# An encoder block with two head groups on one core: the fourth tile of x turned by VectorE's blocks and a trip over DRAM

## What is computed

```python
h = rmsnorm(x, norm_mix[l])                       # x: (1, 1024, 1024)
proj = jnp.einsum('bsd,dc->bsc', h, w_in[l])
qa, ka, va, ga, cq, ckv, kr, gb = jnp.split(proj, split_idx, axis=-1)
...
q = jnp.einsum('bsc,ce->bse', rmsnorm(cq, q_a_norm[l]), w_uq[l])
kv = jnp.einsum('bsc,ce->bse', rmsnorm(ckv, kv_a_norm[l]), w_ukv[l])
k_rope = apply_rope(kr.reshape(B, S, 1, B_ROPE), cos, sin)[:, :, 0, :]
```

## Time and profile before

| | us |
|---|---|
| median of 3 runs | 606.72 (605.74 to 607.55) |
| the profiled execution | 606.28 |
| its span in the trace | 604.4 |
| PE busy | 595.3 (98% of the span) |
| DVE busy | 446.4 (74%) |
| ACT busy | 356.3 (59%) |
| POOL busy | 292.4 (48%) |
| DMA queue of SP | 101.25 MB, 56.2% of 16 engines' span |
| granted clock of TensorE | full in all slices but the last |

### The profile page before, as it was taken

One profiled execution on the slowest core, in us unless ns is written; L12 is line 12 of the kernel. 1 busy time (PEld: TensorE's weight loads), 2 busy tenths in 40 slices (PEclk: granted clock), 3 DMA queues, 4 the chain that ended last, 5 costly groups with the idle time before them and its releaser, 6 DMA issues.

```text
span 604.4 us, 9197 instructions
## 1 busy us (share of the span) xinstructions
PE 595.3 (98%) x3076; PEld 484.0 (80%) x3076; DVE 446.4 (74%) x802; ACT 356.3 (59%) x762; POOL 292.4 (48%) x273
## 2 busy tenths in 40 slices
PE   8999999999999999999999999999999999999996
PEld 7888888788888888888887777777777777888885
DVE  5777663334434439898899788998998988799884
ACT  6644223213333228777787678788788788524563
POOL 4610702515656532536556537677677776510601
PEclk9999999999999999999999999999999999999998
DMA  7587457774776720101015967767768745598042
GB/s 246 190 287 203 155 166 242 230 259 149 245 262 226 224 69 1 36 1 36 2 27 114 242 157 185 190 179 191 192 172 199 203 127 182 177 386 326 1 173 107
DMA packets 72431, 102.11 MB, mean 169 GB/s; under 512 B 10232, under 2 KB 43008, under 8 KB 72384
## 3 DMA queue, kind: packets, MB, share of 16 engines
q1 hardware_dynamic: 72224, 101.25, 56.2%
q10 hardware_dynamic: 160, 0.27, 0.1%
HBM read 60.17 MB, written 31.62 MB: 152 GB/s over the span
## 4 chain that ended last, share of the span: by engine, by line
PE 78%; DMA 8%; DVE 5%; ACT 3%; POOL 2%; SPq 2%; issue 1%; ACTq 0%; DVEq 0%
PE ps L1824 13%; PE ps L1826 13%; PE ps L1825 13%; PE ps L2118 9%; PE ps L2096 7%; PE ps L2026 5%; PE ps L2031 5%; PE ps L1996 3%; PE ps L2046 2%; DMA lat_scratch<-lat_b 2%; PE ps L2006 2%; DMA lat<-lat_scratch 2%; PE ps L1983 2%; PE ps L1982 2%; PE ps L2007 2%; DMA ukv_raw<-w_ukv 1%
## 5 line engine op out<-in xcount | busy, mean ns | idle before, releaser
L1674 DVE TENSOR_TENSOR pT_lo<-ps,pT_hi 128x512 fp32r<-128x512 f32 x102 | 69.3, 684 | 21.5 <-ACT pT_hi L1237 20.3
L1824 PE MATMUL ps<-hT_hi,w_hi 128*128 128x512 f32 x208 | 84.0, 404 | 0.0
L1826 PE MATMUL ps<-hT_hi,w_lo 128*128 128x512 f32 x208 | 81.4, 391 | 0.0
L1825 PE MATMUL ps<-hT_lo,w_hi 128*128 128x512 f32 x208 | 81.1, 390 | 0.0
L1224 ACT ACTIVATE p_b<-ps,stat 128x1024 f32<-128x1024 f32 x64 | 71.3, 1114 | 12.6 <-DVE stat L1649 12.2
L1649 DVE TENSOR_REDUCE stat<-ps 128x1 f32<-128x1024 f32 x64 | 76.5, 1212 | 2.2 <-PE ps L2046 2.0
L1237 ACT ACTIVATE pT_hi<-ps 128x512 fp32r<-128x512 f32 x102 | 60.4, 596 | 23.8 <-PE ps L2096 23.5
L2096 PEld LDWEIGHTS ps<-ident,p_b 128*128 128x128 f32 x408 | 48.7, 140 | 17.4 <-issue 5.2
L2096 PE MATMUL ps<-ident,p_b 128*128 128x128 f32 x408 | 62.0, 275 | 0.6 <-DVE pT_lo L1674 0.3
L810 POOL TENSOR_SCALAR p_w<-p_w,stat 128x384 f32<-128x384 f32 (+1 forms) x40 | 24.4, 623 | 55.7 <-DVE stat L1557 55.7
L926 POOL TENSOR_TENSOR pT_lo<-p_land,pT_hi 128x512 fp32r<-128x512 f32 x26 | 33.3, 1286 | 29.5 <-ACT pT_hi L1244 29.5
(11 more groups left out here) (222 smaller groups left out, 1506.2 us busy)
## 6 DMA issues: line engine op xcount, KB each, us to landing
w_raw<-w_in SPq DMA_DIRECT2D x13, 512.0 KB, 4.5
probs_scratch<-p_blk SPq DMA_DIRECT2D x52, 128.0 KB, 2.8
p_land<-probs_scratch SPq DMA_DIRECT2D x13, 512.0 KB, 4.2
x_in<-x SPq DMA_DIRECT2D x8, 512.0 KB, 3.8
wt_raw<-w_out SPq DMA_DIRECT2D x8, 512.0 KB, 4.4
t_scratch<-wt_hi SPq DMA_DIRECT2D x16, 256.0 KB, 2.6
t_scratch<-wt_lo SPq DMA_DIRECT2D x16, 256.0 KB, 2.8
q<-q_h SPq DMA_DIRECT2D x16, 256.0 KB, 3.7
```

Of the source, the lines that this page charges most:

```text
L1674: nc.vector.tensor_tensor(pT_lo[at_], ps[:, 4 + a, :].rearrange("p (k c) -> p k c", c=P), f(pT_hi[at_]), ALU.subtract).then_inc(s_bTl, 1)
L1824: nc.tensor.matmul(o, a_hi, b_hi, start=first, stop=False, skip_group_check=goes_on)
L1825: nc.tensor.matmul(o, a_hi, b_lo, start=False, stop=False, skip_group_check=goes_on)
L1826: return nc.tensor.matmul(o, a_lo, b_hi, start=False, stop=last, skip_group_check=goes_on)
```

## The change

- `X_PE` goes from 4 to 3: tile 3 is no longer turned on TensorE but by `turn_blocks(3)`, `store_x(3)` and `fetch_x(3)`, and lands in `latT_hi[:, 4, :]`. `turn_x(3)` leaves TensorE's program.
- The buffers alternate by t % 2, so tile 3 writes `x_blk1`, and tiles 4 and 6 `x_blk0`. `x_blk0` moves from 147 KB (where `lat` lies) to 201 KB. `lat_norm(0)` no longer waits until the blocks of an x tile are stored, and `lat_norm(1)` waits for those of tile 7 (`x_blk1` lies where `lat_b1` does) as before, counted anew.
- ScalarE: `h_hi(3)` stands behind the last weight split, ahead of `square_x(6)`; `h_hi(4)` ahead of `lat_stats(0)`.
- VectorE: `h_lo(3)` stands behind `turn_blocks(5)` (before: behind `turn_blocks(4)`); `h_lo(4)` ahead of `lat_norm(0)` (before: behind it).
- SP: `store_x(3)` ahead of `load_x(6)`; `g_q` and `g_kv` behind `load_x(6)`; `fetch_x(3)` ahead of `store_x(4)`; `fetch_x(4)` ahead of `store_x(5)`.

```diff
-X_PE = 4
+X_PE = 3
...
-        x_blk = [at(f"x_blk{i}", kb, [P, 4, KT, Q32]) for i, kb in enumerate((147, 161))]
+        x_blk = [at(f"x_blk{i}", kb, [P, 4, KT, Q32]) for i, kb in enumerate((201, 161))]
...
         def x_turned(t):
-            a, r = ((latT_hi, 0), (latT_hi, 2), (latT_lo, 0), (latT_lo, 2))[t - X_PE]
+            if t == X_PE:
+                return f(latT_hi[:, 4, :]).rearrange("p (r c) -> p r c", r=2)
+            a, r = ((latT_hi, 0), (latT_hi, 2), (latT_lo, 0), (latT_lo, 2))[t - X_PE - 1]
...
+            store_x(3)
             load_x(6)
+            sp.dma_start(g_q[:, :], q_a_norm.partition_broadcast(P)).then_inc(s_glat, 16)
+            sp.dma_start(g_kv[:, :], kv_a_norm.partition_broadcast(P)).then_inc(s_glat, 16)
+            fetch_x(3)
             store_x(4)
             load_x(7)
+            fetch_x(4)
             store_x(5)
-            fetch_x(4)
             store_x(6)
             fetch_x(5)
             store_x(7)
...
             square_x(4)
-            h_hi(3)
             wn_hi_k(6)
             square_x(5)
             wn_hi_k(7)
+            h_hi(3)
             square_x(6)
             square_x(7)
+            h_hi(4)
             lat_stats(0)
-            h_hi(4)
...
                     lat_lo(t - 2)
                     dve.wait_ge(s_latT, t - 1)
-                else:
-                    dve.wait_ge(s_xsto[t], 128)
+                elif t == 1:
+                    dve.wait_ge(s_xsto[1], 192)
...
             for t in range(X_PE, NT):
                 norm_x(t)
                 turn_blocks(t)
-                if t == 4:
+                if t == 5:
                     h_lo(3)
+            h_lo(4)
             lat_norm(0)
-            h_lo(4)
...
             both(2, range(4))
-            turn_x(3)
```

More of the change, by code:

```diff
@@ L236, in encoder @@
         s_wnh, s_wnr = sem("wn_hi_ready"), sem("wn_ready")
-        s_grow, s_gcol, s_gT, s_gb = sem("g_row_in"), sem("g_col_ready"), sem("g_turned"), sem("g_broadcast")
+        s_grow, s_gcol, s_gT, s_gb = sem("g_row_then_fourth_tile_in"), sem("g_col_ready"), sem("g_turned"), sem("g_broadcast")
         s_pA, s_pB = sem("natA_done"), sem("natB_done")
@@ L438, in _ @@
             load_wn(7)
-            sp.dma_start(g_q[:, :], q_a_norm.partition_broadcast(P)).then_inc(s_glat, 16)
-            sp.dma_start(g_kv[:, :], kv_a_norm.partition_broadcast(P)).then_inc(s_glat, 16)
             def store_x(t):
@@ L450, in fetch_x @@
                 sp.dma_start(x_turned(t), xt_scr[t - X_PE].rearrange("a p (r q) c -> (a p) r (q c)", r=2)) \
-                    .then_inc(s_xq[t - X_PE], 16)
+                    .then_inc(s_xq[t - X_PE - 1] if t > X_PE else s_grow, 16)
+            store_x(3)
             load_x(6)
+            sp.dma_start(g_q[:, :], q_a_norm.partition_broadcast(P)).then_inc(s_glat, 16)
+            sp.dma_start(g_kv[:, :], kv_a_norm.partition_broadcast(P)).then_inc(s_glat, 16)
+            fetch_x(3)
             store_x(4)
             load_x(7)
+            fetch_x(4)
             store_x(5)
-            fetch_x(4)
             store_x(6)
@@ L1000, in h_hi @@
                 if t >= X_PE:
-                    act.wait_ge(s_xq[t - X_PE], 16)
+                    act.wait_ge(s_xq[t - X_PE - 1], 16) if t > X_PE else act.wait_ge(s_grow, 32)
                     for r in range(2):
@@ L1443, in _ @@
             h_lo(0, range(1, 2))
-            for t in range(1, 4):
+            for t in range(1, X_PE):
                 norm_x(t)
-                if t < 3:
-                    h_lo(t)
+                h_lo(t)
             def turn_blocks(t):
```

## The result

| | before | after |
|---|---|---|
| median of 6 runs, us | 606.57 (605.42 to 607.55) | 612.33 (609.09 to 614.05) |
| ratio, 95% interval | | 1.0097 (1.0074 to 1.0121) |
| the profiled execution, us | 606.28 | 609.09 |
| its span | 604.4 | 607.2 |
| its mean granted clock | | 0.998 |

What follows compares the result with a forecast made beforehand. Up to 109 us TensorE's work and the DMA-trip chain were taken as nearly equal bounds. The chain starting 3.3 us later, 2.8 carried less 0.25 slack, added 2.5 to 606.28; forecast 609.0, range 606.0 to 611.3.

Steps and rivals of the forecast that it cites:

- the bound: Up to 109 us, TensorE's work and the DMA-trip chain nearly equal; the chain has almost no slack.
- the direction: Whole kernel slower, 609.0 us forecast; chance of slower by more than 0.3% put at 0.54.
- TensorE's 0.80 us: turn_x(3) removed from TensorE's path: natural(3) could start at 38.4, 0.80 earlier; most eaten by a wait before natural(4).
- T3: Landing of tile 3's trip (store, then fetch): 36.1 us, between 34.8 and 37.5.
- T3 + 10.7 = 46.8: Reciprocal of lat_norm(0), after ScalarE's and VectorE's work behind tile 3's landing: 46.8 instead of 43.51, 3.3 us later.
- Rival 3: Waits pile up as turn_blocks(7) waits for tile 5's stores behind fetch_x(4): 611.3 us, decides from T3 above 37; 14 in 100.
- the carry: First latents to job 8: delay of 2.05 to 3.3, taken as 2.8, less 0.25 slack, 2.5 us at job 8.
- The sum: Whole kernel: 606.28 + 2.5 = 608.8 us profiled, 609.2 on the median, given as 609.0.
- 0.7 ahead of `natural(4)`: TensorE waits 0.7 us until lat_norm(0) has read its banks at 47.9, eating most of the 0.80 saved.
- some 2.5 us more at job 8: TensorE's added wait at job 8 for the late chain, with nothing beyond the existing wait at the k jobs.

Runs made afterwards that it cites:

- the trip made and not used: Changed kernel making all of tile 3's trip, while TensorE turns tile 3 again and h_hi(3), h_lo(3) read PSUM at their old places; 610.97 us, 1.0063.
- both orders taken back: Changed kernel with fetch_x(4) back behind store_x(5) and tile 6's square, norm and blocks ahead of tile 3's hi and lo parts; 609.27 us, 1.0049.
- the two put-in waits: Kernel before with four, or two, copies on VectorE ahead of the last latT_lo, so TensorE waits at job 8; 610.46 us (1.0053) and 607.08 us (1.0008).
- their filled one: Kernel before with the four VectorE copies, TensorE filling the wait at job 8 with 28 turns of the identity; 608.40 us, 1.0032.
- x_blk0's place: Kernel before with only x_blk0 moved to 201 KB and lat_norm(0)'s wait for tile 6's stores removed; 606.05 us, 1.0001.
- the fifth tile's order: Kernel before with only h_hi(4) put ahead of lat_stats(0) and h_lo(4) ahead of lat_norm(0); 607.51 us, 1.0011.
- the two filled kernels: Changed kernel with TensorE's two new waits filled by unread transposes, 610.73 us (1.0063); kernel before with its four-copy wait filled likewise, 608.40 us (1.0032).
- the kernel with its waits filled: Changed kernel, TensorE filling its new waits with identity transposes, 14 inside natural(3) and 24 ahead of job 8; 610.73 us, 1.0063.

## Why the prediction was right or wrong

**Right: the bound and the direction.** TensorE's 0.80 us bought nothing, the chain of DMA trips set the end of the first sixth, and the change made it later. That the profiled execution, at 609.09, lies beside the forecast of 609.0 is luck: its job 8 came 3.9 later and not 2.5, it took back 1.1 of this by the end of the span, and it is the one run of six whose mean clock shows no fall.

**Almost right: T3.** 36.87 for 36.1, inside its 34.8 to 37.5. The stores landed at 31.11 (forecast 30.9), the fetch took 5.7 us (5.2). The estimate from the figures of the Trainium skill ("DMA: Bandwidth & Descriptors", section on the anatomy of one DMA), 32.3, is 4.6 us too early; that section's fit is for DMAs issued by GpSimd, and here SP issues them. `natural(3)` saved 0.32 of 0.80. The prediction saw no wait for it; `hT_lo(3)` ends at 37.53 + 1.29 = 38.82, so it could not have started before, but TensorE had by then lost 0.37 to the late split of the last weights and waited for `hT_lo(3)` less than 0.1.

**The step that failed: the first latents, T3 + 10.7 = 46.8, "the chain starts 3.3 us later".** They came at 48.22, and the chain started 4.7 later. With the measured T3 the step gives 47.6. It assumed that VectorE's row of work is the only path. Rival 3 had named the other one (`turn_blocks(7)` behind the stores of tile 5, held by `fetch_x(4)`), gave it 14 in 100, and put its threshold at a T3 above 37. It decided already at 36.87. Its stores were under-costed: 5.0 to 5.7 us each, where tile 4's take 6.8 from the first issue (31.50) to the landing (38.27), with tile 3's fetch and the load of tile 7 in flight, and tile 5's 6.1. In the changed kernel these two paths end within a microsecond of each other (VectorE would be free for `turn_blocks(7)` at 44.33, the stores have landed at 45.11), so taking one away can bring back a microsecond at most. A third path was not in the prediction at all: the load of tile 7 takes 6.0 us in the changed kernel and 7.5 with the trip made and not used, for 4.5 before. It decides only with both orders taken back.

**Right in its amount by luck, wrong in its steps: the carry, "2.05 to 3.3, I take 2.8", less 0.25.** The forecast let 0.8 us of the delay go on the way to job 8 (3.3 to 2.5), and 0.8 went (4.7 to 3.9). So job 8 is 1.4 later than forecast because the chain started 1.4 later. But the steps were others. The forecast took off 0.5 because `lat_norm(1)` loses less, and it did (+3.5 where `lat_norm(0)` has +4.7). But the chain goes by tile 0: its fetch, its `latT_lo` (57.90, +4.7 by 53.17) and so the latents of tile 2. The earlier trace rows had shown it, with the fetch of tile 0 followed by the store of tile 2. The store of tile 6's latents is still issued 4.7 later (86.89 by 82.18). The 0.8 goes behind it, where the forecast had 0.25, and 0.7 of it because the latents of tiles 6 and 7 happened to land faster than before (3.7 us from the first issue to the fetch that waits, for 4.2, and 3.7 for 4.0). w_ukv was issued at 96.62 and not at 95.3, the first k job came 3.45 later. From the first reciprocal to job 8 the kernel before takes 52.85 us; the ten others with the same chain (all of the table but the two put-in waits and their filled one) take 52.1 to 54.3, 53.4 in the mean. A start that is 0.9 earlier is lost in this scatter of 2 us, and so is what one path taken away may bring back at job 8: with one execution each, job 8 doesn't order the variants.

**Missing: a term for the clock.** The sum turned waits of TensorE into microseconds one for one. The waits of 1.7 and 2.2 us were forecast in kind (0.7 ahead of `natural(4)`, "some 2.5 us more at job 8"), but a wait like these can bring the granted clock to 0.50 shortly after TensorE resumes, at 1.7 us in each of the six falls that profiled executions show. Clocks of 0.996 or less, which no run of before, of x_blk0's place, of the fifth tile's order or of the two filled kernels has, were found in 5 of 6 runs of after.

**The account.** Measured +5.8 us. The chain is the kernel with its waits filled: ratio 1.0063, +3.8 us (3.0 to 4.7). The clock is the rest, 1.9 us, a little over one fall per run. The intervals of after and of its filled kernel just overlap (1.0074 and 1.0078), so this split is loose; the clocks of after's runs agree with it, as an estimate: a fall of 1.7 in 607 us lowers the mean by 0.003, so 0.998, three times 0.995, 0.992 and 0.991 read as 0, 1, 1, 1, 2 and 2 falls, 2.0 us per run. The prediction had 2.5 for the first and nothing for the second. The range ended at 611.3 for the same reason: rival 3's +5 was all chain.

**What stays open.** Landings of one and the same store scatter (that of tile 6's latents 3.2 to 5.1 us from its first issue to the fetch that waits for it, with the same program around it), and no run shows why. Nor is it shown where the 0.65 us went that the span regains behind the first gate product of the profiled execution, or why the put-in wait, filled, costs 1.7 us by the median (608.40 for 606.68 on its chip) where its job 8 is 3.2 later, or what decides whether the clock falls behind a wait. A kernel without trip traffic and with the old order of fetch and store was not tried.

## What to carry to other kernels

Before costing a moved step, write down every path that reaches the same instruction, SP's row of waits and the loads queued behind the new transfers among them; where several end within a microsecond, the latest one sets the time and removing one shows nothing. And price a new wait of TensorE at its length plus what the clock may cost behind it (here 1.7 us, behind six of the eleven new waits of 1.67 to 3.88 us in profiled executions), and do not take the profiled execution for the median until its granted clock has been set beside that of the other runs.
